# Moving the first chunk's split, the tables and the norm steps of block one, and identity turns of TensorE in five waits

## The reference

```python
def rms_norm(x, g):
    xf = x.astype(jnp.float32)
    y = xf * lax.rsqrt(jnp.mean(xf * xf, axis=-1, keepdims=True) + EPS)
    return (y * g.astype(jnp.float32)).astype(x.dtype)
```

## Time and profile before

| what | before |
|---|---|
| median of 3 runs | 1814.18 us (1813.52 to 1814.74) |
| the profiled execution | 1810.41 us |
| its span, first to last instruction | 1808.6 us |
| mean granted clock of PE | 0.961 |
| PE busy | 1626.6 us, 90% |
| DVE busy | 1089.2 us, 60% |
| ACT busy | 745.4 us, 41% |

### The profile page before, as it was taken

One profiled execution on the slowest core, in us unless ns is written; L12 is line 12 of the kernel. 1 busy time (PEld: TensorE's weight loads), 2 busy tenths in 40 slices (PEclk: granted clock), 3 DMA queues, 4 the chain that ended last, 5 costly groups with the idle time before them and its releaser, 6 DMA issues.

```text
span 1808.6 us, 25889 instructions
## 1 busy us (share of the span) xinstructions
PE 1626.6 (90%) x10546; PEld 1278.2 (71%) x10546; DVE 1089.2 (60%) x1544; ACT 745.4 (41%) x974; POOL 0.2 (0%) x4
## 2 busy tenths in 40 slices
PE   6999989998999989999999899858789999997776
PEld 5777779997887779998887676534468767653433
DVE  5776768787785768778577663222165975512124
ACT  3556535544546635554456631101034565311111
POOL 0000000000000000000000000000000000000000
PEclk9999999998999999999999899989889999999888
DMA  6552535554563345563654398999956336999996
GB/s 206 183 186 93 175 117 199 196 180 157 170 192 117 125 145 189 183 207 127 214 164 139 108 412 350 412 418 412 410 174 208 129 108 259 376 414 416 413 416 244
DMA packets 174271, 422.54 MB, mean 234 GB/s; under 512 B 15984, under 2 KB 68568, under 8 KB 157528
## 3 DMA queue, kind: packets, MB, share of 16 engines
q1 hardware_dynamic: 174168, 421.07, 63.7%
HBM read 419.99 MB, written 1.05 MB: 233 GB/s over the span
## 4 chain that ended last, share of the span: by engine, by line
PE 63%; DMA 15%; DVE 13%; ACT 4%; issue 3%; SPq 3%; DVEq 0%; ACTq 0%
PE lot L288 16%; PE lot L289 15%; PE lot L290 15%; DVE w_lo L258 4%; PE lot L2217 3%; DMA raw<-w_exp_up 3%; SPq L2114 3%; DMA e_hi<-w_exp_down 3%; ACT w_hi L253 2%; PE lot L2291 2%; DMA two_e_gates<-w_exp_up 1%; DMA e_lo<-w_exp_up 1%; DMA e_hi<-w_exp_up 1%; DMA two_e_sqT<-w_exp_up 1%; PE lot L415 1%
## 5 line engine op out<-in xcount | busy, mean ns | idle before, releaser
L258 DVE TENSOR_TENSOR w_lo<-raw,w_hi 128x2048 fp32r<-128x2048 f32 (+4 forms) x194 | 431.6, 2230 | 119.7 <-ACT w_hi L253 119.0
L253 ACT ACTIVATE w_hi<-raw 128x2048 fp32r<-128x2048 f32 (+4 forms) x194 | 361.3, 1866 | 137.2 <-PE lot L290 121.8
L288 PE MATMUL lot<-one_hT_hi,w_hi 128*128 128x256 f32 x704 | 200.7, 285 | 4.8 <-DVE one_hT_lo L381 4.8
L289 PE MATMUL lot<-one_hT_lo,w_hi 128*128 128x256 f32 x704 | 200.5, 285 | 0.0
L290 PE MATMUL lot<-one_hT_hi,w_lo 128*128 128x256 f32 x704 | 200.3, 285 | 0.0
L288 PE MATMUL lot<-w_hi,two_hT_hi 128*128 128x512 f32 (+1 forms) x448 | 178.1, 398 | 5.6 <-DVE two_hT_lo L381 4.2
L290 PE MATMUL lot<-w_hi,two_hT_lo 128*128 128x512 f32 (+1 forms) x448 | 173.6, 387 | 0.0
L289 PE MATMUL lot<-w_lo,two_hT_hi 128*128 128x512 f32 (+1 forms) x448 | 173.4, 387 | 0.0
L288 PE MATMUL lot<-w_hi,one_hT_hi 128*128 128x512 f32 (+2 forms) x384 | 151.3, 394 | 15.7 <-DVE w_lo L258 7.0
L289 PE MATMUL lot<-w_lo,one_hT_hi 128*128 128x512 f32 (+2 forms) x384 | 147.0, 383 | 0.0
L290 PE MATMUL lot<-w_hi,one_hT_lo 128*128 128x512 f32 (+2 forms) x384 | 146.8, 382 | 0.0
(11 more groups left out here) (429 smaller groups left out, 3166.3 us busy)
## 6 DMA issues: line engine op xcount, KB each, us to landing
raw<-w_in SPq DMA_DIRECT2D x78, 1024.0 KB, 5.0
raw<-ffn_w_up SPq DMA_DIRECT2D x44, 1024.0 KB, 5.1
raw<-ffn_w_down SPq DMA_DIRECT2D x22, 1024.0 KB, 5.0
raw<-w_out SPq DMA_DIRECT2D x16, 1024.0 KB, 6.2
raw<-w_exp_gate SPq DMA_DIRECT2D x14, 1024.0 KB, 18.1
raw<-w_exp_up SPq DMA_DIRECT2D x14, 1024.0 KB, 20.6
two_e_gates<-w_exp_up SPq DMA_DIRECT2D x12, 1024.0 KB, 19.2
e_hi<-w_exp_up SPq DMA_DIRECT2D x10, 1024.0 KB, 21.8
```

The source lines that it names most:

```text
L253: act.activation(K.hi[:, r, 0:n], self.raw(name)[:, 0:n], ACT.Copy).then_inc(K.sig["hi_ready"], 1)
L258: dve.tensor_tensor(K.lo[:, r, 0:n], self.raw(name)[:, 0:n], K.hi[:, r, 0:n].bitcast(F32), ALU.subtract).then_inc(K.sig["lo_ready"], 1)
L288: pe.matmul(out, a[0], b[0], start=start, stop=False)
L289: pe.matmul(out, a[0], b[1], start=False, stop=False)
```

## The change

Seven things are edited, all in the order of the lists, and none in what is computed.

1. The last two down steps (9 and 10) add into the same two lots in PSUM (`down_two`; `part` is the inner loop of `down` with a flag for the start and the end of the sum), so DVE no longer adds step 9 to x by itself.
2. ACT makes the high part of the next layer's first chunk (lat0, or ik of block two) before the last high half of the hidden columns.
3. At n1, root 0 stands before the split of lat0, and the high part of tile 0 before lat1 and root 1; DVE's low part of tile 0 moves between the statistics of tile 1's halves.
4. In layer 0, x tile 1 is loaded behind lat0, and the tables behind gq0 rather than pool1; the sines are taken before the copy of gq.
5. At n2, PE makes the last output product before it transposes tile 0, ACT splits G0 before root 0, and DVE's low part of tile 0 moves from between the additions to behind the scaling of tile 1.
6. `keep_awake` lets PE transpose the identity into the lot it has just claimed: 24 and 18 turns before the latent product of layers 0 and 1, 34 and 32 turns at n2 of each layer, 12 before ik of the first block two. The 36 warm turns before the second block two are gone.
7. The lots at the start of block one are numbered anew, since the last sums now lie in lots 2 and 3.

```diff
 def ffn_ends(steps):
-    return {f"U{e}": f"H{e}" for e in range(steps)} | {f"D{e}": f"Y{e}t1" for e in range(steps)}
+    return {f"U{e}": f"H{e}" for e in range(steps)} | {f"D{e}": f"Y{e}t1" for e in range(steps) if e != steps - 2}
...
     order = [("H0", 0)]
-    for e in range(1, steps):
+    for e in range(1, steps - 1):
         order += [(f"H{e}", e % 2), (f"Y{e - 1}t0", 2), (f"Y{e - 1}t1", 3)]
-    return order + [(f"Y{steps - 1}t0", (steps - 1) % 2), (f"Y{steps - 1}t1", steps % 2)]
+    e = steps - 1
+    return order + [(f"H{e}", e % 2), (f"Y{e}t0", 2), (f"Y{e}t1", 3)]
...
+    def down_two():
+
+        e = steps - 1
+        pe.wait_ge(K.sig["h_lo"], K.sig.at("h_lo", e))
+        for t in range(T):
+            lot = L.claim(pe, f"Y{e}t{t}")
+            for n in range(2):
+                last = part(e - 1, lot, t, n, stop=False)
+        ST.done(last, f"D{e - 1}")
+        pe.wait_ge(K.sig["h_lo"], K.sig.at("h_lo", e + 1))
+        for t in range(T):
+            lot = L.use[f"Y{e}t{t}"][0]
+            part(e, lot, t, 0, start=False).then_inc(K.sig["last_half"], 1)
+            part(e, lot, t, 1, start=False).then_inc(L.filled(f"Y{e}t{t}"), 1)
...
     def step(e, i):
         hidden(e + 1, i)
-        down(e, i)
-
+        if i is None and e == steps - 2:
+            down_two()
+        else:
+            down(e, i)
...
     ST.split_hi(act, f"D{e}")
     tail()
+    if after:
+        after.ST.hi_to(act, after.first)
     high(e, None)
...
-    e = steps - 1
     tail()
-    for t in range(T):
-        L.wait_filled(dve, f"Y{e - 1}t{t}")
-        L.wait_before(dve, f"Y{e - 1}t{t}")
-        add(e - 1, None, t).then_inc(L.drained(f"Y{e - 1}t{t}"), 1)
-        if t == 0:
-            low(e, None)
-
-
+    low(steps - 1, None)
+
+
+
+LATENT_TURNS = (24, 18)
+SECOND_NORM_TURNS = (34, 32)
+INDEX_TURNS = 12
...
+def keep_awake(K, pe, lot, turns):
+
+    for _ in range(turns):
+        pe.transpose(K.ps[lot][:, 0, 0:P], K.ident[:, :], K.ident[:, :])
...
-    order = [("xTt0", 2), ("xTt1", 3), ("lat", 0), ("gkv", 2), ("gq", 3), ("cT", 1), ("q0", 2), ("q1", 0), ("kv0", 1),
+    order = [("xTt0", 1), ("xTt1", 0), ("lat", 2), ("gkv", 1), ("gq", 0), ("cT", 3), ("q0", 2), ("q1", 1), ("kv0", 0),
...
         if before is None:
-            for t in range(T):
-                sp.dma_start(K.x[:, t, :], A["x"][0][t * P:(t + 1) * P, :]).then_inc(sig[f"x_in{t}"], 16)
+            sp.dma_start(K.x[:, 0, :], A["x"][0][0:P, :]).then_inc(sig["x_in0"], 16)
...
-            if tables and name == "pool1":
+            if before is None and name == "lat0":
+                sp.dma_start(K.x[:, 1, :], A["x"][0][P:S, :]).then_inc(sig["x_in1"], 16)
+            if tables and name == "gq0":
+                load_tables(nc, A, sig, tables, sp)
                 sp.dma_start(K.rope[:, :, :], A["c_rope"]).then_inc(sig["rope_in"], 16)
-                load_tables(nc, A, sig, tables, sp)
...
         transpose_tile(K, L, pe, M.tmp, "xTt0", 0, sig, "n1_normed")
-        L.claim(pe, "lat")
+        keep_awake(K, pe, L.claim(pe, "lat"), LATENT_TURNS[before is not None])
         L.wait_drained(pe, "xTt0")
...
         ST.done(out_part(0, 1, 1), "wo01")
+        out_part(1, 1, 1).then_inc(L.filled("wot1"), 1)
         transpose_tile(K, L, pe, M.tmp, "fTt0", 0, sig, "n2_normed")
-        out_part(1, 1, 1).then_inc(L.filled("wot1"), 1)
+        keep_awake(K, pe, L.claim(pe, "fTt1"), SECOND_NORM_TURNS[0])
         transpose_tile(K, L, pe, M.tmp, "fTt1", 1, sig, "n2_normed")
+        keep_awake(K, pe, L.claim(pe, "H0"), SECOND_NORM_TURNS[1])
...
         act.activation(st[:, 232:233], K.ident[:, 0:1], ACT.Sqrt)
+        if before:
+            ST.hi_to(act, "lat1")
+        root_act_of(K, act, "n1", 0)
         ST.hi_to(act, "lat0")
-        root_act_of(K, act, "n1", 0)
+        tile_hi(0)
         ST.hi_to(act, "lat1")
         root_act_of(K, act, "n1", 1)
-        tile_hi(0)
         tile_hi(1)
...
         ST.hi_to(act, "ukv")
+        if tables:
+            rotation_sines(sig, tables, act)
         take("gq", M.lat[:, :, C_GQ:C_GK], lambda ps: ps[:, :, :])
...
+        ST.hi_to(act, "G0")
         root_act_of(K, act, "n2", 0)
-        ST.hi_to(act, "G0")
         act_hi(K, L, act, "fTt0", M.hT_hi[:, :, 0:P], lambda lot: by_feature(K, lot))
         ST.hi_to(act, "U0")
         root_act_of(K, act, "n2", 1)
...
         if before:
             ST.lo_to(dve, "lat0")
-        first_stats(0)
+        first_stats(0, 0)
+        first_stats(0, 1)
         rms_var(K, dve, link, "n1", 0)
         rms_scale(K, dve, link, "n1", 0, M.tmp, M.gain)
-        first_stats(1)
+        ST.lo_to(dve, "lat0")
+        first_stats(1, 0)
+        tile_lo(0)
+        first_stats(1, 1)
         rms_var(K, dve, link, "n1", 1)
-        ST.lo_to(dve, "lat0")
-        tile_lo(0)
         rms_scale(K, dve, link, "n1", 1, M.tmp, M.gain)
...
-        add_halves(1)
+        add_half(1, 0)
+        stats_of(K, dve, 1, 0)
+        add_half(1, 1)
+        link(stats_of(K, dve, 1, 1))
         rms_var(K, dve, link, "n2", 1)
         rms_scale(K, dve, link, "n2", 1, M.tmp, M.gain)
+        low_tile(0)
         ST.lo_to(dve, "G0")
         low_tile(1)
+        ST.lo_to(dve, "U0")
         ST.lo_to(dve, "G1")
...
-        if before:
-            E.warm(pe, SEAM_TURNS)
-        else:
+        if ahead:
             ahead.L.wait_drained(pe, f"Y{FF_STEPS - 1}t0")
...
-        L.claim(pe, "ik")
+        lot = L.claim(pe, "ik")
+        if ahead:
+            keep_awake(K, pe, lot, INDEX_TURNS)
```

74 lines of the change are left out of this document (33 added, 41 removed).

## The result

The changed kernel took 1792.7 us (median of 4 executions, 1790.07 to 1795.56) against 1813.85 for the kernel before (4 executions): 0.9878 of its time, 95% interval 0.986 to 0.9896. The forecast was 1798.2 with a range of 1793.5 to 1804.5; the direction was right, the gain 21 us instead of 16, and the median lay 0.8 us under the range. The profiled execution took 1795.56 us (span 1793.8), against 1810.41 (1808.6): 14.85 us less, where 15.95 had been summed.

The account below looks back on a forecast made before the run. PE, busy in 90% of the span, was taken as the bound, with time only in its idle or slow-clock stretches. Terms 4.1 + 5.9 - 0.7 + 5.0 + 0.55 + 1.1 = 15.95 us gave 1798.2 us, range 1793.5 to 1804.5.

Parts of the forecast that it names:

- The start: Start of layer 0: root first and lat0 landing at 10.3 bring first product and gkv 4.1 us earlier; bounds 2.9 to 5.0.
- lower case of 9.5: Start of layer 0: lat0 landing at 9.5 instead of 10.3, which would make the gain 5.0 us.
- The tables: Pool projection: loading tables earlier removes PE's 4.34 us wait and 1.61 of slow clock, 5.9 us; bounds 4.3 to 5.9.
- n2: Norm ahead of the feed-forward part: 0.4 us lost each, 0.7 in both layers; per norm 0.5 gained to 1.5 lost.
- The joint of the layers: Between layers 0 and 1: transposes 2.3 us, first product 4.85, gkv 5.0 us earlier; bounds 3.3 to 6.
- rival one: Clock falls in remaining waits at joint of the layers and start, costing 1.7 and 1.6 us; 1802.5 us, chance 0.17.
- The joint to block two: End of block one to ik: earlier h_lo and one DVE addition less gain 0.55 us; bounds 0.2 and 0.9.
- Between the blocks two: Without the 36 warm turns ik starts 1.65 us earlier, 1.1 net of low clock; bounds 1 lost, 2 gained.
- Rival four: Identity turns do not hold the clock and run slowly, costing 19.4 us: 1817.6 us, slower; chance 0.03.
- three signs of being wrong: Turns run at 0.21, lat0 lands as late as before, or the last half add still waits for lat0's low split.
- first three rivals: Clock falls in waits, 0.17; tables or layer joint give half, 0.12; n2 better and lat0 at 9.5, 0.08.
- with the same distance: Step from profiled execution to median: 3.8 us added to the forecast profile of 1794.4, giving 1798.2 us.

Follow-up runs that it names:

- the two runs named above: Changed kernel with the 36 warm turns between the blocks two back, 1794.9 us; changed kernel without the 12 turns ahead of ik, 1798.0 us.
- a_warm_back: Changed kernel with the 36 warm turns between the blocks two back in their place; 1794.9 us, ratio 0.99 to the kernel before.
- before_p2: The kernel before, unchanged, run for a third profile; 1815.6 us.
- a_root_first: Changed kernel with ACT's root of tile 1 ahead of U0's high split at n2, turns 22 and 33; 1791.0 us, ratio 0.9869.

## Why the prediction was right or wrong

**The terms.** The start: 4.1 forecast, 5.5 at the first product and 5.35 at gkv. The order of the chain was right; lat0 landed at 8.9 instead of my 10.3, which went past my own lower case of 9.5. Over the profiles of the changed kernel the first product starts between 14.22 and 16.12, so the term is 3.6 to 5.5 against the first profile of before, and 5.5 was luck. That lat0 lands sooner with tile 1 of x behind it is no luck: its split starts at 8.92 to 10.82 in the 14 profiles that have this edit, at 11.18 to 11.65 in the four that have not. The tables: 5.9 forecast, 5.88 measured, and 5.96 alone; of that 0.4 is lost again within 28 us in both, behind a low split for which PE now waits, a wait that the prediction did not have. n2: 0.7 loss forecast for both layers, 0.5 between the transposes behind the pool projection and the first down step (198.68 us, 198.17 before), but 0.4 of it is that loss ahead of n2. From the transposes behind the next product (209.50 before, 198.63 after) to the down step it is 0.15, and in layer 1 0.12: 0.3 in both layers. The mechanism, the split ahead of the root, was shown by taking it away. The joint of the layers: 5.0 forecast, 3.53 measured (10.72 ahead at the first down step, 14.25 at gkv). The steps were right, 2.3 to the transposes and 2.75 more at the first product, but the clock falls between 434 and 438, as rival one has it, 1.5 us where I had put 1.7. Without that fall, as in the two runs named above, the joint would give the forecast 5.0. The joint to block two: 0.55 forecast, 0.47 measured to ik's start; then the fall behind ik takes 1.6 us, which I had not counted. Between the blocks two: 1.65 forecast for ik's start, 1.65 measured (11.77 to 10.12 us behind the last product), and 0.94 for the second group against 1.1. That is this pair: in the other two profiles of the kernel before ik starts 13.23 and 10.25 us behind, as PE's sequencer stands longer or shorter ahead of the warm turns, and the rest of the span takes back what was won (a_warm_back).

**Rival four** is refuted: at n2 the turns run at 0.11 us each and the clock stays at 1.00, and without turns the kernel is 6.4 us slower. What the Trainium skill, TensorE: Matmul & The Clock Gate, says in Part 4: PE-mode transpose of the full clock and transposes does not hold here, so the trust in this trace over that sentence was right. Of rival one's evidence, the 1.00 behind 1.51 us at 858.69 was one execution: in another of the same kernel (before_p2) the clock fell there. None of the three signs of being wrong came, though the forecast missed: the half add at 420.28 still stands right behind the low split, but PE had ended its half of the product only at 420.24. A slip of adding: the chances of the forecast and the first three rivals make 0.92, not 0.93.

**The number.** Up to the second group behind ik the changed kernel is 13.05 us ahead by the two first profiles, 1.8 less than the terms to there sum to; at the end it is 14.85 ahead, 1.1 less than the whole sum. That the end is so near is partly luck: from that second group to the experts' last product, where nothing was moved, the changed kernel gains another 4.75 us (452.23 against 456.98), and behind the last block's second group it loses 3.94 (470.01 against 466.07). The step that failed is the one from the profile to the median, "with the same distance": I put the distance of 3.8 us between one execution and the median of three onto a kernel whose profile turned out to lie 2.9 above its median of four. 3.8 and 2.9, less the 1.1 by which the profile fell short, are the 5.5 us between forecast and median; the distance of one execution from a median is noise, and it does not carry over. Means of 47 and 12 executions give 1813.5 and 1795.0, a gain of 18.5 (1.0), and 1795.0 is inside the range. The profile of before was 3.1 us under its kernel's mean, at a granted clock of 0.961 where 17 others had 0.958. The range was made with "the noise of the median, 1 us each way", where executions of one program reach 4.4 to 6.5 us to either side of their mean; the median of the first four lay 0.8 us beyond the range.

**What stays open.** The three profiled executions of before (mean 1813.6) and the four of the changed kernel (1797.9, two of them from the slower chip) differ by 15.6 us, and up to the second group behind ik by 14.6, where the terms to there sum to 14.85, though single terms were off by 1 to 2 us either way. The eight executions of the changed kernel of which only the time, the span and the mean clock are known have a mean of 1793.6. So the 2.5 us between the forecast gain and that of all means lie in executions that no view shows, and no place can be named for them; in those that have one, the stretches of the blocks two differ by up to 6 us between profiles of the same program. That these differences are the clock's is shown behind ik and, by the busy time of the same matmuls, for the two stretches of the first block two shown above; for the rest the mean clock goes with the time, and no run isolates what begins a fall. Two edits of n2, the last output product ahead of the transposes and the moved low part of tile 0, were not run alone.

## What to carry to other kernels

A root or another 0.2 us step that others wait for belongs ahead of a 2 us split in an engine's list; it was worth 1.4 us in each layer. The counts of filler turns have to be fitted to it: by an estimate from 0.11 us for a turn, 34 instead of 22 would have reached 0.9 us past the start of the next transposes at 230.52 of a_root_first. Turns of the identity held the clock at n2, where PE stands 4.08 and 3.25 us without them, and bought 2.1 and 1.9 us there; at the joint of the layers, where it stands 0.79 and 2.42 us without them, they bought nothing, and ahead of the last block what they gave and took came to nothing in the time. And before a range is put around a forecast of one percent, look at how far executions of the same program lie apart; a profile is one of them.

## What the hardware showed that I had not expected

The clock falls in a PE that is busy without a gap: 4.40 of 4.40 us at a mean of 0.61, right behind 24 matmuls of 72 columns that ran at full clock (2.68 us). Whether this fall happens differs between executions of one program whose starts agree within 0.5 us, and the next 460 us can take 5 us more or less in the same program, at a granted clock of 0.93 or 0.95. The transfer of lat0 landed 1.9 us apart in two executions of the same program. And PE's sequencer stands 2.3 to 3.1 us at or among the identity turns ahead of the second block two in four profiles, with 36 and with 20 of them, and only 0.3 to 0.5 us in two others.
